# Expert weights found in groups of four, TensorE's expert products two steps later, in a hybrid decoder step

## The chip, the core and the metric

One core of a Trainium2 chip runs the whole program. The metric is the device time of one execution in microseconds (us). The engines are TensorE (PE in the profile; PEld is its weight load), VectorE (DVE), ScalarE (ACT), GpSimd (POOL) and SyncE (SP); SyncE and GpSimd issue the DMAs of this kernel, and 16 DMA engines carry them.

## The reference, cut to what matters

The program is one layer of a decoder for 512 prompt tokens and 8 running sequences. It has a modulated RMSNorm, a combined projection, gated-DeltaNet and forgetting attention, an output projection, and then PEER, a layer with 16384 experts of which each token and each of 8 heads picks 16. The change is in PEER alone, which computes this:

```
q = (xb @ wq).reshape(blk, PEER_HEADS, 2, PEER_DK_HALF)
s = jnp.einsum('thpc,hpnc->thpn', q, subkeys).astype(jnp.float32)
sv, si = lax.top_k(s, PEER_TOPK)
...
fv, fi = lax.top_k(cand, PEER_TOPK)
eidx = jnp.take_along_axis(cidx, fi, axis=-1)
gate = jax.nn.softmax(fv, axis=-1)
act = jax.nn.gelu(jnp.einsum('thkd,td->thk', pu[eidx], xb).astype(jnp.float32), approximate=False) * gate
return jnp.einsum('thk,thkd->td', act.astype(xb.dtype), pv[eidx])
```

So for each token, head and pick, a row of `pu` (1024 numbers) is multiplied with the token and summed, the sum goes through GELU and is scaled by the gate, and the row of `pv` (1024 numbers) times that weight is added to the token's output. The rows of `pu` and `pv` lie side by side in one table, `peer_uv`, 8 KB for an expert.

## The kernel before, in words

The expert stage starts at about 946 us of the span and lasts to its end. The prompt is cut into 4 tiles of 128 tokens, one token on each partition. A unit is one tile and one head (32 units, `UNITS`), and a step is one of the 16 picks of a unit; a further unit of 8 steps, `SAMPLES`, one for each running sequence, stands after unit 27. That makes 520 steps, listed in `steps_`. `events` is the loop that each engine writes out for itself: event e is step e for GpSimd's lookahead, VectorE and ScalarE, and TensorE does step e - `BEHIND` in it.

One step g goes through the engines like this:

- GpSimd, `gather(g)`, L2006: one indirect DMA brings 128 rows of 8 KB (1 MB, `u` and `v` of 128 experts) into buffer g % 8 of `UV`. Six of the 8 buffers lie in the tile RING, the last two in R, which is how the trace names them: the names alone tell which of the 8 steps a row belongs to. From `gather(8)` on, it waits for `v_used` to reach g - 7: TensorE must be through with step g - 8.
- VectorE, `dot(g)`, L1786 (L1784 for the samples): waits for the gather to land, multiplies `u` with the token's row `H2` and sums it (one instruction and the read of its accumulator).
- ScalarE, `gelu(q)`, L1098 (L1096): GELU over the dots of a group of steps, 128x2.
- VectorE, `weigh(q)`, L1804 (L1801): that times the gate, 128x2, which gives the semaphore `weights`.
- ScalarE, `diagonal(g)`, L1108: the identity scaled by the weight column, a 128x128 matrix in one of 4 places of `DG`; it waits for `weights`.
- TensorE, `value_step(g)`, L413: diagonal times `v`, two products 128x512, summed over a whole tile (8 units) in two PSUM banks. Its last matmul raises `v_used`. The samples (`sample_step`) need no diagonal: they multiply the matrix `AM`, whose columns `weigh` fills, with `v`.

All loops are written out, and each engine's queue is in the order of the program. In event e VectorE does `dot(e)`, then in even events `weigh` of steps e - 2 and e - 1, then some of the top-16 search of the unit after the next (`picks`), and here and there a norm. ScalarE in odd events does `gelu` of steps e - 1 and e, then the diagonals of steps e - 3 and e - 2. TensorE does `value_step(e - 4)` and then the slot of event e, if there is one.

Slots (`post_slots`, `slots_at`) are the other work of this stage: for tiles 1 to 3 the output projection (`wo`, two products 128x512 in a slot), the turning of the normed tokens (`turn`), the query projection (`wq`) and the scores. One slot goes with one event: they lie at events 56 to 109 (tile 1), 184 to 237 (tile 2) and 301 to 366 (tile 3, with the samples' rows). SyncE loads their weights, 2 MB at a time, in that region. Outside it TensorE has the expert products alone.

At the end of a tile, `sums_out` on VectorE (event 7 after the last step of the tile) waits for the last product of that tile.

Of the kernel before, what the change touches and what calls it, by code (L numbers as in the profile page):

```python
# [8 lines left out]
ALU = mybir.AluOpType  # L9
ACT = mybir.ActivationFunctionType  # L10
# [25 lines left out]
def hybrid_decoder_step(nc, a, o):  # L36

    ctx = ExitStack()
    with ctx:
        sems = {}  # L40

        def S(name):
            if name not in sems:
                sems[name] = ctx.enter_context(nc.semaphore(name))
            return sems[name]
# [24 lines left out]
        def part(_t, _at, _n, /, **dims):  # L70
            v = _t[:, _at:_at + _n]
            if not dims:
                return v
            names = list(dims)
            return v.rearrange(f"row ({' '.join(names)}) -> row {' '.join(names)}", **{k: dims[k] for k in names[1:]})
# [105 lines left out]
        GTT = R1[:, 11880:11888]  # L181
        DOTS = R1[:, 11888:11896]
        AM = R1[:, 11896:11960]
        EIX = R2[:, 11264:11328].bitcast(U32).rearrange("q (t n) -> q t n", t=4)
        FVS = part(R2, 11328, 64, t=4, n=16)
        DOT = part(R2, 11392, 64, t=4, n=16)
        AG = part(R2, 11456, 64, t=4, n=16)
        GAT = part(R2, 11520, 64, t=4, n=16)
# [88 lines left out]
        def take_bank(job, pool):  # L277

            n = taken[pool]
            taken[pool] += 1  # L280
            size = len(pools[pool])
            b = pools[pool][n % size]
            if n >= size:
                nc.tensor.wait_ge(S(f"bank{b}_free"), n // size)
            job_of[job] = (b, n // size + 1)
            newest[0] = job
            return banks[b]
# [104 lines left out]
        units = list(range(28)) + [SAMPLES] + list(range(28, UNITS))  # L392
        steps_ = [(n, s_) for n in units for s_ in range(NB if n == SAMPLES else STEPS)]
        at_step = {step_: g for g, step_ in enumerate(steps_)}
        AHEAD, BEHIND = 3, 4
        events = range(len(steps_) + BEHIND)

        def step_at(e):

            return steps_[e] if 0 <= e < len(steps_) else (None, None)  # L400

        def slots_of(e):

            n, s_ = step_at(e)
            return slots_at.get(n * STEPS + s_, ()) if n is not None and n < SAMPLES else ()
# [5 lines left out]
        def _(pe):  # L411
            def mm(out, lhsT, rhs, start=True, stop=True, sem=None, **k):
                i = nc.tensor.matmul(out, lhsT, rhs, start=start, stop=stop, **k)  # L413
                if sem is not None:
                    i.then_inc(sem, 1)
                return i
# [38 lines left out]
            for t in range(5):  # L455
                n = P if t < 4 else NB
# [409 lines left out]
                mm(hi[:, :], DG[:, k % 4, :], UV[g % UN][:, 1536:2048], first, last, S("v_used"))  # L866

            def sample_step(g, t):
                pe.wait_ge(S("weights"), g // 2 + 1)
                if t == 0:  # L870
                    take_bank(("ys", 0), "D")
                    take_bank(("ys", 1), "D")
                pe.wait_ge(S(f"uv_in{g % UN}"), 16 * (g // UN + 1))
                for half in range(2):
                    mm(banks[job_of["ys", half][0]][0:NB, :], AM[:, t * 8:t * 8 + 8], UV[g % UN][:, 1024 + half * 512:1536 + half * 512], t == 0, t == NB - 1,
                       S("v_used") if half else None)

            for e in events:
                g = e - BEHIND
                n, s_ = step_at(g)  # L880
# [14 lines left out]
        def _(act):  # L895
            A = nc.scalar.activation
# [9 lines left out]
            for t in range(5):  # L906
                n = P if t < 4 else NB
# [145 lines left out]
            def root(name, t):  # L1053
                n = P if t < 4 else NB
                act.wait_ge(S("sumsq"), nth_norm(name) + 1)
                A(SS[0:n, 5 + t:6 + t], SS[0:n, t:t + 1], ACT.Sqrt, scale=1.0 / D_MODEL, bias=EPSB[0:n, :]).then_inc(S("root"), 1)
# [31 lines left out]
            def gates(n):  # L1088
                act.wait_ge(S("picked"), n + 1)
                A(GAT[:, n % 4, :], FVS[:, n % 4, :], ACT.Exp, bias=NMX[:, n % 4:n % 4 + 1], accum_out=SUMG[:, n % 4:n % 4 + 1]).then_inc(S("gate_raw"), 1)  # L1090

            def gelu(q):
                n, s_ = steps_[2 * q]
                act.wait_ge(S("dots"), 2 * q + 2)
                if n == SAMPLES:
                    A(DOTS[:, s_:s_ + 2], DOTS[:, s_:s_ + 2], ACT.Gelu).then_inc(S("gelu"), 1)  # L1096
                else:
                    A(AG[:, n % 4, s_:s_ + 2], DOT[:, n % 4, s_:s_ + 2], ACT.Gelu).then_inc(S("gelu"), 1)  # L1098

            def diagonal(g):  # L1100
                n, s_ = steps_[g]
                if n == SAMPLES:
                    return
                k = n * STEPS + s_
                act.wait_ge(S("weights"), g // 2 + 1)
                if k >= 4:
                    act.wait_ge(S("v_used"), at_step[divmod(k - 4, STEPS)] + 1)
                A(DG[:, k % 4, :], ident[:, :], ACT.Copy, scale=AG[:, n % 4, s_:s_ + 1]).then_inc(S("diagonal"), 1)  # L1108
# [20 lines left out]

            for e in events:  # L1130
                n, s_ = step_at(e)
                if e % 2:
                    if n is not None:
                        gelu(e // 2)
                    for g in (e - 3, e - 2):
                        if 0 <= g < len(steps_):
                            diagonal(g)
                if n is not None and n + 1 < UNITS and s_ == 6:
                    gates(n + 1)
                if n is not None and n % PH == 0 and 0 < n < SAMPLES and s_ == 9:  # L1140
                    root(f"f{n // PH - 1}", n // PH - 1)
                if (n, s_) == (29, 9):
                    root("f4", 4)
                if (n, s_) == (25, 6):
                    act.wait_ge(S("sample_picks"), 1)
                    A(GT64[0:64], FV64[0:64], ACT.Exp, bias=MX64[0:64], accum_out=SUM64[0:64]).then_inc(S("sample_exp"), 1)
                for slot_ in slots_of(e - 1):
                    post_slot(*slot_)
# [4 lines left out]
        def _(dve):  # L1153
            V = nc.vector
# [614 lines left out]
            def unit_picks(n):  # L1769

                if n + 2 < UNITS:
                    yield from prompt_picks(n + 2)
                if n == 24:
                    yield from sample_picks()
# [20 lines left out]

            def weigh(q):

                n, s_ = steps_[2 * q]
                dve.wait_ge(S("gelu"), q + 1)
                if n == SAMPLES:  # L1800
                    V.tensor_tensor(AM[:, 9 * s_:9 * s_ + 10:9], DOTS[:, s_:s_ + 2], GTT[:, s_:s_ + 2], ALU.mult).then_inc(S("weights"), 1)  # L1801
                else:
                    ag = AG[:, n % 4, s_:s_ + 2]
                    V.tensor_tensor(ag, ag, GAT[:, n % 4, s_:s_ + 2], ALU.mult).then_inc(S("weights"), 1)  # L1804

            def sums_out(t):

# [64 lines left out]
            for e in events:  # L1872
                n, s_ = step_at(e)
                if n is not None:
                    dot(e)
                if e % 2 == 0 and 0 <= e // 2 - 1 < len(steps_) // 2:
                    weigh(e // 2 - 1)
                if n is not None and n < SAMPLES:
                    if s_ == 4:
                        for _ in picking:  # L1880
                            pass
                        picking = unit_picks(n)
                    for _ in range(2 if 0 <= n * STEPS + s_ - 24 * STEPS - 4 < STEPS else 1):
                        next(picking, None)
                    if s_ == 8 and n + 1 < UNITS:
                        gate_scale(n + 1)
                    if n and n % PH == 0:
                        if s_ == 6:
                            sums_out(n // PH - 1)
                        elif s_ == 7:  # L1890
                            residual(n // PH - 1)
                        elif s_ == 11:
                            finish(n // PH - 1)
                    if n == 25 and s_ == 8:
                        sample_gates()
                    if n == 26 and s_ == 4:
                        sample_indices()
                    if n == 29:
                        if s_ == 6:
                            sample_sums()  # L1900
                        elif s_ == 7:
                            residual(4)
                        elif s_ == 11:
                            finish(4)
                for slot_ in slots_of(e - 1):
                    post_slot(*slot_)
# [449 lines left out]
```

## Time and profile before

| what | value |
|---|---|
| time, median of 3 runs | 2443.9 us (2438.39 to 2452.11) |
| time of the profiled execution | 2435.51 us |
| its span | 2433.2 us |
| TensorE matmul busy | 1916.3 us, 79% |
| VectorE busy | 1415.4 us, 58% |
| ScalarE busy | 502.3 us, 21% |
| GpSimd busy | 866.0 us, 36% |
| DMA rate in the expert stage | 364 to 420 GB/s in the slices of the page, but for the last |

The span runs from the first to the last instruction; the profiled execution's own time has 2.3 us around it. In a row of the timeline the columns are: start in us, duration in us, engine, line, operation, tile written and tile read, shapes, how many instructions were merged, and in brackets how long the engine was idle before them and what ended that.

### The profile page before, as it was taken

How to read it: one execution, taken by the hardware profiler on the slowest of the kernel's cores; microseconds unless marked ns; L12 is line 12 of the kernel's file. 1: busy time of each engine (PE TensorE's matmuls, PEld its weight loads, DVE VectorE, ACT ScalarE, POOL GpSimd, SP SyncE). 2: the span in 40 equal slices, each digit the busy share in tenths (PEclk: the TensorE clock that was granted, in tenths of full speed). 3: DMA queues.
4: the chain of work that ended last, by engine and by line, in shares of the span. 5: the costliest groups of instructions: out<-in, count | busy, mean ns of one | idle time of the engine just before them, and what ended most of it. 6: DMA issues, size and time to landing. Idle time of an engine off the chain costs nothing.

```text
span 2433.2 us, 24921 instructions
## 1 busy us (share of the span) xinstructions
PE 1916.3 (79%) x7976; PEld 1050.7 (43%) x7976; DVE 1415.4 (58%) x3274; ACT 502.3 (21%) x1312; POOL 866.0 (36%) x642
## 2 busy tenths in 40 slices
PE   2799976785899887778886778886788997776776
PEld 1364433454777766323552323542232552222222
DVE  2200686668555524676656776656776667865764
ACT  0111211111212112222221222222222222211221
POOL 0000263795123201343443443334443344443442
PEclk6789985556999998899999899999999999999999
DMA  7022342764345457999999999999999999999997
GB/s 283 18 70 75 123 163 65 231 198 158 105 139 174 156 179 272 366 420 406 416 415 409 398 413 402 416 416 415 393 408 364 383 410 416 388 417 420 397 380 294
DMA packets 168930, 728.32 MB, mean 299 GB/s; under 512 B 17789, under 2 KB 18782, under 8 KB 102098
## 3 DMA queue, kind: packets, MB, share of 16 engines
q0 software_dynamic: 75024, 545.82, 55.1%
q1 hardware_dynamic: 93778, 180.92, 21.9%
q8 instruction: 65, 1.06, 0.2%
q14 instruction: 63, 0.52, 0.1%
HBM read 720.69 MB, written 6.08 MB: 299 GB/s over the span
## 4 chain that ended last, share of the span: by engine, by line
PE 41%; DMA 31%; DVE 13%; issue 6%; POOL 4%; ACT 2%; SPq 2%; another core or an unknown queue 0%; DVEq 0%; ACTq 0%; POOLq 0%
PE bank L413 39%; DMA RING<-in_peer_uv,R 20%; DMA R<-in_peer_uv,R 8%; DVE RING L1786 3%; SPq L2020 1%; POOL R L1934 1%; PE bank L420 1%; DVE R L1786 1%; ACT R L1108 1%; DMA R<-h2s_d 1%; DVE RING L1319 1%; POOL MV L1934 1%; DMA R<-in_x_sample 1%; POOL R L1951 0%; DMA R<-in_x_prompt 0%
## 5 line engine op out<-in xcount | busy, mean ns | idle before, releaser
L413 PE MATMUL bank<-RING,R 128*128 128x512 f32 (+1 forms) x1560 | 756.0, 625 | 227.0 <-ACT R L1108 217.1
L2006 POOL DMA_INDIRECT RING<-in_peer_uv,R x390 | 439.3, 1126 | 759.5 <-PE bank L413 653.0
L413 PE MATMUL bank<-R 128*128 128x128 f32 (+5 forms) x2248 | 491.3, 372 | 95.4 <-ACT R L1108 68.0
L413 PEld LDWEIGHTS bank<-RING,R 128*128 128x128 f32 (+1 forms) x1560 | 287.5, 195 | 629.8 <-issue 616.7
L413 PEld LDWEIGHTS bank<-R 128*128 128x128 f32 (+2 forms) x2248 | 302.1, 194 | 253.4 <-issue 226.8
L1786 DVE SCALAR_TENSOR_TENSOR RING<-RING,R 128x1024 f32<-128x1024 f32 x192 | 235.0, 1225 | 172.5 <-DMA RING<-in_peer_uv,R 171.8
L1786 DVE SCALAR_TENSOR_TENSOR RING<-RING,MV 128x1024 f32<-128x1024 f32 x192 | 235.0, 1224 | 155.3 <-DMA RING<-in_peer_uv,R 153.5
L1098 ACT ACTIVATE R<-R 128x2 f32<-128x2 f32 x256 | 52.1, 203 | 1051.4 <-DVE RING L1786 844.6
L2006 POOL DMA_INDIRECT R<-in_peer_uv,R x130 | 149.1, 1147 | 204.8 <-PE bank L413 200.7
L1108 ACT ACTIVATE R<-ident,R 128x128 f32<-128x128 f32 x512 | 173.6, 386 | 0.5 <-PE bank L413 0.2
L420 PE MATMUL bank<-ident,R 128*128 128x128 f32 (+2 forms) x310 | 64.0, 351 | 137.1 <-ACT R L996 54.5
L413 PEld LDWEIGHTS bank<-HT,R 128*128 128x128 f32 x1024 | 134.7, 197 | 47.0 <-issue 45.9
L1984 POOL TENSOR_TENSOR R<-R,level 128x512 f32<-128x512 f32 x56 | 80.1, 1453 | 198.3 <-DVEq L1601 144.0
L413 PE MATMUL bank<-HT,RING 128*128 128x512 f32 (+1 forms) x336 | 150.5, 602 | 0.0
L413 PE MATMUL bank<-HT,R 128*128 128x128 f32 (+1 forms) x1024 | 135.7, 282 | 0.7 <-issue 0.7
L1786 DVE SCALAR_TENSOR_TENSOR R<-R,MV 128x1024 f32<-128x1024 f32 x64 | 78.4, 1225 | 66.9 <-DMA R<-in_peer_uv,R 66.5
L1934 POOL TENSOR_TENSOR R<-R,RING 128x2048 f32<-128x2048 f32 x20 | 90.5, 4532 | 73.3 <-DMA R<-in_cache_k 73.1
L420 PEld LDWEIGHTS bank<-ident,R 128*128 128x128 f32 (+2 forms) x310 | 49.0, 188 | 154.6 <-ACT R L996 57.3
L1786 DVE SCALAR_TENSOR_TENSOR R<-R 128x1024 f32<-128x1024 f32 x64 | 78.2, 1223 | 60.3 <-DMA R<-in_peer_uv,R 60.2
L413 PE MATMUL bank<-RING,HT 128*8 128x128 f32 (+5 forms) x768 | 111.2, 352 | 2.1 <-ACT HT L1050 2.1
L413 PE MATMUL bank<-R,HT 128*128 128x64 f32 (+2 forms) x288 | 96.0, 478 | 3.1 <-DVE HT L1378 3.1
L1927 POOL DMA_INDIRECT RING<-in_cache_logf,small x1 | 1.3, 1289 | 269.1 <-PE bank L413 269.1
(295 smaller groups left out, 1820.8 us busy)
## 6 DMA issues: line engine op xcount, KB each, us to landing
R<-in_peer_wq SPq DMA_DIRECT2D x16, 2048.0 KB
RING<-in_w_mod SPq DMA_DIRECT2D x12, 2048.0 KB, 8.3
R<-in_cache_v SPq DMA_DIRECT2D x84, 256.0 KB, 3.2
R<-in_cache_k SPq DMA_DIRECT2D x80, 256.0 KB, 4.0
MV<-in_cache_k SPq DMA_DIRECT2D x48, 256.0 KB, 3.6
R<-in_w_out SPq DMA_DIRECT2D x6, 2048.0 KB
MV<-in_cache_v SPq DMA_DIRECT2D x44, 256.0 KB, 3.2
RING<-in_w_in SPq DMA_DIRECT2D x5, 2048.0 KB, 8.6
```

What stands on the lines that cost most here:

```text
L413: i = nc.tensor.matmul(out, lhsT, rhs, start=start, stop=stop, **k)
L420: i = nc.tensor.transpose(out, in_, ident[0:n, 0:n])
L1098: A(AG[:, n % 4, s_:s_ + 2], DOT[:, n % 4, s_:s_ + 2], ACT.Gelu).then_inc(S("gelu"), 1)
L1108: A(DG[:, k % 4, :], ident[:, :], ACT.Copy, scale=AG[:, n % 4, s_:s_ + 1]).then_inc(S("diagonal"), 1)
L1319: V.tensor_reduce(SC[:, :, n // 4, (n % 4) * 4:(n % 4) * 4 + 4].rearrange("p h g -> p g h"), pages(n).rearrange("p g (h d) -> p g h d", d= ...
L1786: V.scalar_tensor_tensor(u, u, 1.0, H2[n // PH % 2], ALU.mult, ALU.mult, accum_out=DOT[:, n % 4, s_:s_ + 1]).then_inc(S("dots"), 1)
L1927: nc.gpsimd.indirect_dma_start(LG, None, a["cache_logf"][0].rearrange("n p h -> n (p h)"), bass.IndirectOffsetOnAxis(ap=PTI, axis=0)).then ...
L1934: T(k, k, QB[:, n // 4 % 2:n // 4 % 2 + 1, :].to_broadcast([P, 4, 512]), ALU.mult).then_inc(S("kprod"), 1)
L1984: T(M, AT, level[:, lv:lv + 1, :].to_broadcast([P, 4, P]), ALU.mult).then_inc(S(f"level{hb}"), 1)
L2006: nc.gpsimd.indirect_dma_start(UV[g % UN], None, a["peer_uv"][0], bass.IndirectOffsetOnAxis(ap=idx, axis=0)).then_inc(S(f"uv_in{g % UN}"), 16)
L2020: sp.dma_start(dst, src, **k).then_inc(S(sem), 16)
```

## The change

GELU, gate product and diagonals go in groups of four steps (`GROUP = 4`) in place of two. The gelu of steps 4q to 4q+3 stands in ScalarE's event 4q+3, the `weigh` of that group in VectorE's event 4q+4 behind `dot(4q+4)`, and the four diagonals in ScalarE's event 4q+5. `BEHIND` is 6 in place of 4, so TensorE's `value_step(g)` stands in event g + 6, behind the slots of events up to g + 5. The number of `UV` buffers (8) and of `DG` places (4), and all that the other engines do, stay.

```diff
--- before.py
+++ after.py
@@ -392,7 +392,8 @@
         units = list(range(28)) + [SAMPLES] + list(range(28, UNITS))
         steps_ = [(n, s_) for n in units for s_ in range(NB if n == SAMPLES else STEPS)]
         at_step = {step_: g for g, step_ in enumerate(steps_)}
-        AHEAD, BEHIND = 3, 4
+        AHEAD, BEHIND = 3, 6
+        GROUP = 4
         events = range(len(steps_) + BEHIND)
 
         def step_at(e):
@@ -866,7 +867,7 @@
                 mm(hi[:, :], DG[:, k % 4, :], UV[g % UN][:, 1536:2048], first, last, S("v_used"))
 
             def sample_step(g, t):
-                pe.wait_ge(S("weights"), g // 2 + 1)
+                pe.wait_ge(S("weights"), g // GROUP + 1)
                 if t == 0:
                     take_bank(("ys", 0), "D")
                     take_bank(("ys", 1), "D")
@@ -1090,19 +1091,19 @@
                 A(GAT[:, n % 4, :], FVS[:, n % 4, :], ACT.Exp, bias=NMX[:, n % 4:n % 4 + 1], accum_out=SUMG[:, n % 4:n % 4 + 1]).then_inc(S("gate_raw"), 1)
 
             def gelu(q):
-                n, s_ = steps_[2 * q]
-                act.wait_ge(S("dots"), 2 * q + 2)
+                n, s_ = steps_[GROUP * q]
+                act.wait_ge(S("dots"), GROUP * q + GROUP)
                 if n == SAMPLES:
-                    A(DOTS[:, s_:s_ + 2], DOTS[:, s_:s_ + 2], ACT.Gelu).then_inc(S("gelu"), 1)
+                    A(DOTS[:, s_:s_ + GROUP], DOTS[:, s_:s_ + GROUP], ACT.Gelu).then_inc(S("gelu"), 1)
                 else:
-                    A(AG[:, n % 4, s_:s_ + 2], DOT[:, n % 4, s_:s_ + 2], ACT.Gelu).then_inc(S("gelu"), 1)
+                    A(AG[:, n % 4, s_:s_ + GROUP], DOT[:, n % 4, s_:s_ + GROUP], ACT.Gelu).then_inc(S("gelu"), 1)
 
             def diagonal(g):
                 n, s_ = steps_[g]
                 if n == SAMPLES:
                     return
                 k = n * STEPS + s_
-                act.wait_ge(S("weights"), g // 2 + 1)
+                act.wait_ge(S("weights"), g // GROUP + 1)
                 if k >= 4:
                     act.wait_ge(S("v_used"), at_step[divmod(k - 4, STEPS)] + 1)
                 A(DG[:, k % 4, :], ident[:, :], ACT.Copy, scale=AG[:, n % 4, s_:s_ + 1]).then_inc(S("diagonal"), 1)
@@ -1129,10 +1130,10 @@
 
             for e in events:
                 n, s_ = step_at(e)
-                if e % 2:
-                    if n is not None:
-                        gelu(e // 2)
-                    for g in (e - 3, e - 2):
+                if e % GROUP == GROUP - 1 and n is not None:
+                    gelu(e // GROUP)
+                if e % GROUP == 1:
+                    for g in range(e - 5, e - 1):
                         if 0 <= g < len(steps_):
                             diagonal(g)
                 if n is not None and n + 1 < UNITS and s_ == 6:
@@ -1795,13 +1796,13 @@
 
             def weigh(q):
 
-                n, s_ = steps_[2 * q]
+                n, s_ = steps_[GROUP * q]
                 dve.wait_ge(S("gelu"), q + 1)
                 if n == SAMPLES:
-                    V.tensor_tensor(AM[:, 9 * s_:9 * s_ + 10:9], DOTS[:, s_:s_ + 2], GTT[:, s_:s_ + 2], ALU.mult).then_inc(S("weights"), 1)
+                    V.tensor_tensor(AM[:, 9 * s_:9 * s_ + 28:9], DOTS[:, s_:s_ + GROUP], GTT[:, s_:s_ + GROUP], ALU.mult).then_inc(S("weights"), 1)
                 else:
-                    ag = AG[:, n % 4, s_:s_ + 2]
-                    V.tensor_tensor(ag, ag, GAT[:, n % 4, s_:s_ + 2], ALU.mult).then_inc(S("weights"), 1)
+                    ag = AG[:, n % 4, s_:s_ + GROUP]
+                    V.tensor_tensor(ag, ag, GAT[:, n % 4, s_:s_ + GROUP], ALU.mult).then_inc(S("weights"), 1)
 
             def sums_out(t):
 
@@ -1873,8 +1874,8 @@
                 n, s_ = step_at(e)
                 if n is not None:
                     dot(e)
-                if e % 2 == 0 and 0 <= e // 2 - 1 < len(steps_) // 2:
-                    weigh(e // 2 - 1)
+                if e % GROUP == 0 and 0 <= e // GROUP - 1 < len(steps_) // GROUP:
+                    weigh(e // GROUP - 1)
                 if n is not None and n < SAMPLES:
                     if s_ == 4:
                         for _ in picking:
```

## Rows read from the trace of the kernel before

**Rows 1.** The page: busy time of the engines, and the chain of waits.

```profile
PE 1916.3 (79%) x7976; PEld 1050.7 (43%) x7976; DVE 1415.4 (58%) x3274; ACT 502.3 (21%) x1312; POOL 866.0 (36%) x642
...
PE 41%; DMA 31%; DVE 13%; issue 6%; POOL 4%; ACT 2%; SPq 2%; another core or an unknown queue 0%; DVEq 0%; ACTq 0%; POOLq 0%
```

**Rows 2.** Busy time by window: the five stretches without slots.

```profile
core 0: us, PE busy (x) PEld busy (x) DVE busy (x) ACT busy (x) POOL busy (x), PEclk, DMA share, GB/s
1011.10:1112.50 101.40, 76.16 (x162) 29.92 (x161) 69.50 (x189) 24.65 (x72) 42.65 (x40) 0.97 1.01 416
1283.00:1474.70 191.70, 140.34 (x288) 55.20 (x287) 130.13 (x351) 46.04 (x131) 81.11 (x72) 0.95 1.00 407
1644.80:1804.90 160.10, 115.02 (x240) 45.30 (x239) 109.24 (x295) 38.35 (x109) 67.14 (x60) 0.96 1.00 407
2012.30:2221.30 209.00, 151.29 (x324) 59.16 (x323) 154.04 (x433) 49.59 (x145) 86.22 (x80) 0.98 0.99 410
2271.60:2407.80 136.20, 99.38 (x210) 39.45 (x209) 84.61 (x203) 29.27 (x89) 60.05 (x52) 0.96 0.99 403
```

**Rows 3.** The same view: the query slots of tiles 1 to 3, and tile 3's output slots.

```profile
1164.50:1283.00 118.50, 102.20 (x428) 61.26 (x428) 71.06 (x196) 26.36 (x87) 49.30 (x40) 1.00 1.02 415
1499.50:1644.80 145.30, 124.19 (x497) 71.98 (x496) 89.57 (x239) 36.50 (x109) 57.49 (x49) 1.00 1.02 415
1897.30:2012.30 115.00, 108.53 (x476) 66.43 (x475) 71.09 (x197) 29.47 (x92) 48.55 (x41) 1.00 1.01 407
1804.90:1897.30 92.40, 82.41 (x200) 31.15 (x199) 61.11 (x152) 24.10 (x60) 30.27 (x27) 0.96 0.94 361
```

**Rows 4.** Timeline: one round of the buffers where nothing else runs.

```profile
2377.95 1.23 DVE L1786 SCALAR_TENSOR_TENSOR RING<-RING,MV 128x1024 f32<-128x1024 f32 x1 [1.26 <-DMA RING<-in_peer_uv,R]
2379.10 0.16 DVE L1804 TENSOR_TENSOR R<-R 128x2 f32<-128x2 f32 x1
2380.42 1.23 DVE L1786 SCALAR_TENSOR_TENSOR RING<-RING,MV 128x1024 f32<-128x1024 f32 x1 [1.16 <-DMA RING<-in_peer_uv,R]
2381.69 0.20 ACT L1098 ACTIVATE R<-R 128x2 f32<-128x2 f32 x1 [4.17 <-DVE RING L1786]
2381.80 0.68 ACT L1108 ACTIVATE R<-ident,R 128x128 f32<-128x128 f32 x2
2382.33 3.67 PE L413 MATMUL bank<-R 128*128 128x512 f32 x8 [1.29 <-ACT R L1108]
2384.55 0.94 POOL L2006 DMA_INDIRECT R<-in_peer_uv,R  x1 [2.10 <-PE bank L413]
...
2392.84 1.23 DVE L1786 SCALAR_TENSOR_TENSOR R<-R,MV 128x1024 f32<-128x1024 f32 x1 [1.25 <-DMA R<-in_peer_uv,R]
```

**Rows 5.** Timeline: a round whose gather was issued late.

```profile
2350.77 0.68 ACT L1108 ACTIVATE R<-ident,R 128x128 f32<-128x128 f32 x2
2351.30 8.89 PE L413 MATMUL bank<-RING,R 128*128 128x512 f32 x16 [2.75 <-ACT R L1108]
2354.84 1.81 POOL L2006 DMA_INDIRECT RING<-in_peer_uv,R  x1 [4.62 <-PE bank L413]
2363.04 1.23 DVE L1786 SCALAR_TENSOR_TENSOR RING<-RING,MV 128x1024 f32<-128x1024 f32 x1 [2.25 <-DMA RING<-in_peer_uv,R]
```

**Rows 6.** Timeline: the long wait at a turn slot, and the gather behind it.

```profile
1887.11 0.59 PE L420 MATMUL bank<-ident,R 8*128 8x8 f32 x4 [7.25 <-DVE R L1216]
1891.54 0.94 POOL L2006 DMA_INDIRECT RING<-in_peer_uv,R  x1 [10.48 <-PE bank L413]
1897.27 1.23 DVE L1786 SCALAR_TENSOR_TENSOR RING<-RING,R 128x1024 f32<-128x1024 f32 x1 [3.54 <-DMA RING<-in_peer_uv,R]
```

**Rows 7.** Timeline: the first two gate products of the samples.

```profile
2231.58 0.16 DVE L1801 TENSOR_TENSOR R<-R 128x2 f32<-128x2 f32 x1
2240.72 0.16 DVE L1801 TENSOR_TENSOR R<-R 128x2 f32<-128x2 f32 x1
```

## The prediction

> **What bounds the kernel now.** I read the page first, for shares: no engine is full, and the chain of waits is mostly TensorE and DMA [rows 1]. Then the busy time by window, because the expert stage has two kinds of stretch. Without slots [rows 2] the DMA share is 0.99 to 1.01 at 403 to 416 GB/s, while TensorE is busy three quarters of the time: there the kernel moves bytes. With query slots TensorE is at 85 to 94% and the DMA share is still 1.01 or 1.02; only in tile 3's output slots does the rate fall, to 361 GB/s [rows 3]. Then the timeline of one quiet round, for what keeps the DMA queue filled [rows 4]. The reader is to see a ring there, not a list of busy engines: dot, gelu, diagonals, products, gather, landing, dot.
>
> The ring in numbers [rows 4]. The dot at 2380.42 is the last that the gelu of 2381.69 waits for; the diagonals start at 2381.80 (1.38 us after the dot's start), the products at 2382.33, and the first product done lets a gather go at 2384.55 (2.75 after the diagonals). It goes into a buffer named R, and the first dot on R is at 2392.84, 8.29 later. 1.38 + 2.75 + 8.29 = 12.42 us. How many steps is that? The first diagonal of a pair (step 2q) waits for the dot of step 2q+3, because ScalarE's next gelu stands before it, and it frees the buffer of step 2q+8. So the ring covers five steps: 12.42 / 5 = 2.484 us a step, 1.0486 MB in that time being 422 GB/s. That is the DMA rate; the ring follows it, with slack.
>
> How much slack? A late round shows it [rows 5]: that gather's instruction took 1.81 in place of 0.94 us, started at 2354.84, and its dot came at 2363.04, after VectorE had waited 2.25 us where 1.16 to 1.26 is usual [rows 4], so it was about 1.0 late. 8.20 less the 0.87 of the long instruction is 7.33 us: this is what a gather needs when the queue before it has only just run short. Of the 8.29 of a quiet round about 1 us is waiting in the queue. With the queue wholly run out (GpSimd idle 10.48 before) it took 1897.27 - 1891.54 = 5.73 [rows 6].
>
> **The change: the ring gets shorter by a step.** Step 4q is now weighed behind the dot of step 4q+4, and it frees the buffer of step 4q+8. From dot to dot that is four steps, not five, and the budget at the DMA rate falls from 12.42 to 4 x 2.484 = 9.94 us. What must fit in it: the dot and the gate product behind it, 2379.26 - 2377.95 = 1.31 [rows 4], and about 0.14 to the diagonal, 1.45 in all; gelu is off this path, since it needs dot 4q+3 only. Then 2.75 to the gather; then the landing. With the landing of a quiet round, 8.29, that is 12.5; with 7.33, 11.5; with 5.73, 9.93. So the gather of step 4q+8 comes late once in four steps in all cases but the last. The other three are released 1.8 us apart (3.67 for two steps) where the DMA takes 2.48 for each, so they follow without a gap: one gap in each group.
>
> **TensorE's pauses.** Four steps of products are 2 x 3.67 = 7.3 us in one burst; in a round of 9.94 or more TensorE then has 2.6 us or more of idle time in one piece, where it now has 1.29 twice [rows 4]. The row with 2.75 idle before it has 16 matmuls in 8.89 us in place of 7.3, and its diagonals-to-gather time is 2354.84 - 2350.77 = 4.07, not 2.75 [rows 5]; the granted clock of these stretches is 0.95 to 0.98 [rows 2], so it does fall from 2.4 to 1.2 GHz at times. The ring at the low clock is 1.45 + 4.07 + landing: 11.25 with 5.73, 12.85 with 7.33.
>
> The Trainium skill, "TensorE: Matmul & The Clock Gate", section "Why this matters for your kernels", says to leave no idle gaps between bursts of matmuls, since the clock then goes back to half. That speaks against this change, and the trace agrees in the row with 2.75 idle before it; applied to every burst, the rule is what the second rival supposes.
>
> Which value? Bounds of the round are 9.93 and 12.85. I take the low clock at the start of most bursts (4.07) and a landing of 6.2, between 5.73 and 7.33, because the queue now runs partly out in each round and so comes nearer to the row with the empty queue: 1.45 + 4.07 + 6.2 = 11.7 us a group of four.
>
> The Trainium skill, "DMA: Bandwidth & Descriptors", section "Anatomy of one DMA — SWDGE (gpsimd) path", gives 2.0 us plus the bytes at 436 GB/s for one DMA of this kind, an estimate of 4.4 us for 1 MB. With that the ring would be shorter than 9.94 and nothing would be lost. The rows show 5.73 at the least, so the measurement decides; this is the reason for the third rival.
>
> How many groups? The five stretches without slots are steps 16 to 55, 112 to 183, 240 to 299, 368 to 447 and 464 to 515: 304 steps, 76 groups, and they now last 798.4 us (the five windows' lengths) [rows 2], 10.5 a group; the 0.56 above 9.94 is weight loads and late dots. 76 x 11.7 = 889: plus 91. Ends: 76 x 12.85 = 977, plus 178; and 0 at the other.
>
> **Elsewhere.** Query slots (128 steps, 378.8 us, 11.8 a group) [rows 3]: products and slots alternate, TensorE is nearly full and a ring of 11.7 just fits; where no weights are being loaded it doesn't, so between 0 and 1 us for each of 32 groups; I take half, 15. Tile 3's output slots (28 steps in 92.4 us) [rows 3] are TensorE's own work and don't change. At the samples' turn slot TensorE waits 7.25 us [rows 6]; it has passed two products fewer before that slot, so two gathers fewer are under way: 0 to 5 us, I take 4. Samples: their first four products now wait for the dot of sample 4, whose gate product is at 2240.72 today, where the first pair goes at 2231.58 [rows 7]; the gathers behind them start some 8 us later, but VectorE there waits for the sample rows anyway: 0 to 8, I take 3. Nothing from the 130 gate products that go (0.16 each) and the gelus: VectorE waits over 1 us for DMA in each quiet step [rows 4], and ScalarE is idle 79% [rows 1]. The end of the kernel costs nothing: today's last four products already wait for the last dots. `sums_out` stands seven events behind its last step and TensorE six, so it hardly waits; SyncE's queue waits for dots and norms, which move with the rest, and no instruction of it is moved.
>
> Sum: 2435.5 (the profiled execution) + 91 + 15 + 4 + 3 = 2548.5. The median of the runs shown is 8.4 above that execution, so 2557; I say 2556.
>
> **The rivals.** First, the clock holds: 1.45 + 2.75 + 6.5 = 10.7 a group, plus 15 and perhaps 12 elsewhere, 2471 (before's median plus 27). For it: a gap of 2.6 is not above the 2.75 that fell. Against: any late landing makes the gap longer than 2.75. Chance 0.2.
>
> Second, low clock in every burst and no easing of the landing: 12.85 a group, plus 178 and 22, 2644. Against: an emptier queue landed in 5.73. Chance 0.12.
>
> Third, the ring still fits: landing 5.73 at the full clock, 9.93 against 9.94. Then the round stays at the DMA rate and the time is 2444, no change. It decides at one point: whether VectorE's waits ahead of the dot of step 4q+8 stay at 1.2 us. Chance 0.08.
>
> Fourth, the other side, faster: with the products two steps later, TensorE can begin a slot two events sooner, while it would be idle. In two steps it is idle 1.29 [rows 4]; if each of the three blocks of slots gained that and its waits (7.25 at the longest [rows 6]) shrank, 5 to 15 us would go, 2434. It needs the third as well, since otherwise the ring eats it. Chance 0.05.
>
> **How the numbers follow.** 0.55 for the forecast (2500 to 2610), and the rest as above. Within 0.5% (12 us) is what a measurement of this kernel can't tell from no change: 0.08; faster 0.05; slower 0.87. The range of 8 in 10 is 2468 to 2630: it takes in the first rival and stops short of the bound of 2644.
>
> **What would show it.** In the changed kernel's quiet stretches: one VectorE wait of 2 to 3.5 us in every four dots and three of 1.2; ScalarE's copies in fours every 11 to 12 us; TensorE in bursts of 16 matmuls with 3 to 4 us between them; a DMA rate near 360 GB/s where it is 403 to 416; granted clock clearly below 0.95. Wrong would be: dots still 2.48 apart through a group, or a longer time with the extra in the slot stretches.

## The result and the profile after

The changed kernel takes 2614.6 us (median of 4 runs, 2606.89 to 2615.35), the kernel before 2443.4 in the same comparison: a ratio of 1.0696, 95% interval 1.066 to 1.0732. The profiled execution took 2615.3 us, 179.8 more than that of before.

The page, its busy times and its chain of waits:

```profile
PE 1992.6 (76%) x7976; PEld 1093.9 (42%) x7976; DVE 1409.8 (54%) x3144; ACT 489.1 (19%) x1182; POOL 857.9 (33%) x642
...
PE 40%; DMA 32%; DVE 13%; issue 7%; POOL 3%; ACT 2%; SPq 2%; another core or an unknown queue 0%; DVEq 0%; POOLq 0%; ACTq 0%
```

Against [rows 1], VectorE and ScalarE have 130 instructions fewer each, and the time did not fall for it. TensorE has the same 7976 matmuls and is busy 76 us more: the same work, more of it at the lower clock. The shares of the chain have hardly moved, so they alone wouldn't say what went wrong.

The busy time by window does. First the five stretches without slots (the same steps as in [rows 2]), with their sum:

```profile
1013.10:1132.70 119.60, 84.11 (x163) 34.88 (x164) 68.74 (x179) 23.73 (x62) 45.93 (x40) 0.86 0.91 350
1321.10:1539.90 218.80, 155.49 (x288) 63.88 (x289) 129.36 (x332) 44.38 (x113) 79.02 (x71) 0.84 0.91 347
1725.10:1910.10 185.00, 127.84 (x243) 52.81 (x244) 108.41 (x279) 36.97 (x94) 69.94 (x60) 0.84 0.91 347
2131.50:2376.00 244.50, 169.52 (x322) 69.56 (x322) 152.72 (x413) 47.64 (x125) 89.15 (x80) 0.87 0.91 350
2432.20:2586.20 154.00, 107.64 (x208) 44.22 (x208) 84.06 (x189) 28.11 (x76) 58.76 (x52) 0.89 0.91 352
sum 921.90, PE 644.60 PEld 265.34 DVE 543.29 ACT 180.82 POOL 342.80; mean PE 128.92 PEld 53.07 DVE 108.66 ACT 36.16 POOL 68.56
```

The DMA rate is 347 to 352 GB/s where it was 403 to 416, and the clock 0.84 to 0.89 where it was 0.95 to 0.98. The stretches last 921.9 us in place of 798.4: 123.5 of the 179.8 us are here.

The DMA share, 0.91, has fallen less than the rate. Summed over the five stretches, the DMA engines were busy for some 840 us where some 797 were enough before for about the same bytes. So of the 123.5 us they stood idle in some 81, and for some 42 more the same work took them longer.

Then the query slots of the three tiles and tile 3's output slots, as in [rows 3]:

```profile
1187.80:1321.10 133.30, 108.22 (x416) 63.77 (x416) 70.39 (x186) 25.36 (x77) 45.03 (x40) 0.92 0.98 380
1568.80:1725.10 156.30, 127.59 (x488) 74.47 (x488) 88.54 (x227) 35.18 (x97) 52.53 (x49) 0.93 0.98 388
2012.40:2131.50 119.10, 105.97 (x457) 63.90 (x455) 70.61 (x187) 27.12 (x81) 46.06 (x41) 1.00 1.00 388
1910.10:2012.40 102.30, 86.45 (x215) 34.24 (x214) 60.78 (x144) 24.01 (x54) 28.72 (x28) 0.92 0.88 331
```

The query slots last 408.7 us in place of 378.8, tile 3's output slots 102.3 in place of 92.4.

The timeline of one round, which answers to [rows 4]. The four gathers at the top are those of one group; the first of them is the second row.

```profile
2557.07 1.23 DVE L1787 SCALAR_TENSOR_TENSOR RING<-RING,MV 128x1024 f32<-128x1024 f32 x1 [1.25 <-DMA RING<-in_peer_uv,R]
2557.66 1.44 POOL L2007 DMA_INDIRECT RING<-in_peer_uv,R  x1 [6.26 <-PE bank L414]
2559.41 0.94 POOL L2007 DMA_INDIRECT RING<-in_peer_uv,R  x1 [0.30 <-PE bank L414]
2561.09 0.94 POOL L2007 DMA_INDIRECT R<-in_peer_uv,R  x1 [0.75 <-PE bank L414]
2562.81 0.94 POOL L2007 DMA_INDIRECT R<-in_peer_uv,R  x1 [0.78 <-PE bank L414]
2563.67 1.23 DVE L1787 SCALAR_TENSOR_TENSOR RING<-RING,MV 128x1024 f32<-128x1024 f32 x1 [2.90 <-DMA RING<-in_peer_uv,R]
2564.82 0.16 DVE L1805 TENSOR_TENSOR R<-R 128x4 f32<-128x4 f32 x1
2565.01 1.28 ACT L1109 ACTIVATE R<-ident,R 128x128 f32<-128x128 f32 x4 [4.01 <-DVE R L1805]
2565.56 7.10 PE L414 MATMUL bank<-RING,R 128*128 128x512 f32 x16 [3.02 <-ACT R L1109]
2567.20 1.23 DVE L1787 SCALAR_TENSOR_TENSOR RING<-RING,MV 128x1024 f32<-128x1024 f32 x1 [2.22 <-DMA RING<-in_peer_uv,R]
2567.78 1.45 POOL L2007 DMA_INDIRECT RING<-in_peer_uv,R  x1 [4.04 <-PE bank L414]
...
2574.64 1.23 DVE L1787 SCALAR_TENSOR_TENSOR RING<-RING,MV 128x1024 f32<-128x1024 f32 x1 [1.27 <-DMA RING<-in_peer_uv,R]
...
2576.53 5.37 PE L414 MATMUL bank<-RING,R 128*128 128x512 f32 x8 [3.87 <-ACT R L1109]
```

The dot at 2563.67 is that of step 4q+4. Behind it comes the gate product, and only then do the four scale copies (the diagonals, ScalarE's four merged instructions) run. The gather at 2567.78 brings step 4q+8, whose dot is at 2574.64: 10.97 us for four steps in this good round, where 9.94 is the DMA rate. VectorE's waits of 2.90 and 2.22 us show where the queue had run short, and TensorE stood still for 3.02 us in one piece, then for 3.87; behind the second pause 8 matmuls took 5.37 us, where 3.67 is the high clock [rows 4].

### The profile page after: what moved, and what is told of

Read it like the earlier page. It is cut to its first block, busy times and chain, and to the rows that moved or that the text cites. A ratio compares the mean times of both kernels' runs of the same rounds, so it can differ in the third digit from the quotient of the medians.

```text
span 2612.9 us, 24661 instructions
## 1 busy us (share of the span) xinstructions
PE 1992.6 (76%) x7976; PEld 1093.9 (42%) x7976; DVE 1409.8 (54%) x3144; ACT 489.1 (19%) x1182; POOL 857.9 (33%) x642
## 4 chain that ended last, share of the span: by engine, by line
PE 40%; DMA 32%; DVE 13%; issue 7%; POOL 3%; ACT 2%; SPq 2%; another core or an unknown queue 0%; DVEq 0%; POOLq 0%; ACTq 0%
PE bank L414 38%; DMA RING<-in_peer_uv,R 27%; DVE RING L1787 5%; DMA R<-in_peer_uv,R 2%; ACT R L1109 2%; SPq L2021 1%; POOL R L1935 1%; PE bank L421 1%; DVE RING L1320 1%; POOL MV L1935 1%; DMA R<-h2s_d 1%; DMA R<-in_x_sample 0%; POOL R L1952 0%; POOL R L1951 0%; DMA R<-in_x_prompt 0%
## 5 line engine op out<-in xcount | busy, mean ns | idle before, releaser
L414 PE MATMUL bank<-RING,R 128*128 128x512 f32 (+1 forms) x1560 | 838.0, 687 | 389.0 <-ACT R L1109 372.5
L414 PEld LDWEIGHTS bank<-RING,R 128*128 128x128 f32 (+1 forms) x1560 | 325.9, 219 | 832.1 <-issue 813.8
L414 PE MATMUL bank<-R 128*128 128x128 f32 (+6 forms) x2248 | 485.8, 369 | 28.3 <-ACT R L1071 9.0
L414 PEld LDWEIGHTS bank<-R 128*128 128x128 f32 (+3 forms) x2248 | 302.7, 193 | 169.3 <-issue 143.5
L1109 ACT ACTIVATE R<-ident,R 128x128 f32<-128x128 f32 x512 | 164.6, 390 | 451.5 <-DVE R L1805 434.0
L2007 POOL DMA_INDIRECT R<-in_peer_uv,R x130 | 142.4, 1096 | 143.0 <-PE bank L414 135.3
L1099 ACT ACTIVATE R<-R 128x4 f32<-128x4 f32 x128 | 26.3, 205 | 812.0 <-DVE RING L1787 436.2
L414 PEld LDWEIGHTS bank<-HT,RING 128*128 128x128 f32 (+1 forms) x336 | 62.4, 191 | 80.5 <-issue 80.5
```

The source lines that it names most:

```text
L1099: A(AG[:, n % 4, s_:s_ + GROUP], DOT[:, n % 4, s_:s_ + GROUP], ACT.Gelu).then_inc(S("gelu"), 1)
L2007: nc.gpsimd.indirect_dma_start(UV[g % UN], None, a["peer_uv"][0], bass.IndirectOffsetOnAxis(ap=idx, axis=0)).then_inc(S(f"uv_in{g % UN}"), 16)
```

## The experiments

Two rivals were set against the theory that the ring, from a dot to the dot on the buffer that it frees, is a step shorter: A, TensorE's place behind more slots does it; B, the bursts of 16 matmuls and the low clock behind each pause do it. Ratios are to runs of the kernel before on the same chip, whose own median moved between 2429 and 2443 us; "quiet" is the length of the five stretches without slots in the profiled execution.

**The other half of the change alone.**

```
-        AHEAD, BEHIND = 3, 4
+        AHEAD, BEHIND = 3, 6
```

> The kernel before with BEHIND = 6 and groups of two left as they were: only TensorE's place in the order of the slots moves. Theory (the ring of the buffers is shortened from five steps to four by the group of four): the ring stays at five steps, so the time stays within 0.5% of before, 2431 to 2455 us. Rival A (the order does it: products behind two more slots keep the buffers back): 2490 to 2600 us. Rival B (bursts of four and TensorE's clock): as the theory, 2431 to 2455.

Measured: 2454.0 us, ratio 1.0062 (1.0037 to 1.0087). Quiet 796.8 us against 798.4. The later products cost 0.6%, a little more than the 0.5% that the theory allowed, all of it in the stretches with slots: query slots 387.6 us against 378.8, the blocks with output and turn slots (steps 56 to 71, 184 to 191 and 300 to 327) 179.8 against 169.2. A small cost that the theory had at nothing; rival A is out for the rest.

**The groups of four alone**: the changed kernel with `BEHIND = 4`.

> The changed kernel with BEHIND = 4: groups of four alone. Theory: all of the loss is still there, 2595 to 2630 us. Rival A (the order): most of it goes, 2444 to 2520. Rival B (bursts and clock): 2595 to 2630.

Measured: 2621.9 us, ratio 1.0743 (1.0684 to 1.0802), quiet 922.9. The grouping carries the whole loss. The two halves don't add up: once the group of four is there, the later products cost nothing more. By stretch (one profiled execution of each) the three blocks with output and turn slots take 183.9 us here, 179.8 with the later products alone and 186.3 with both, against 169.2 before; the query slots take 420.8 here and 408.7 with both.

**The group of four, weighed a dot earlier.** One edit to the changed kernel on VectorE:

```
-                if e % GROUP == 0 and 0 <= e // GROUP - 1 < len(steps_) // GROUP:
-                    weigh(e // GROUP - 1)
+                if e % GROUP == GROUP - 1 and e // GROUP < len(steps_) // GROUP:
+                    weigh(e // GROUP)
```

> The changed kernel, but VectorE does the gate product of a group right behind the group's own last dot (4q+3) instead of behind dot 4q+4; bursts of four, BEHIND = 6 and 8 buffers stay. Theory: the ring is five steps again, 12.42 us at the DMA rate, against some 1.7 + 2.75 to 4.1 + 5.6 to 7.3 = 10 to 13 needed, so most of the loss goes: 2440 to 2500 us, the quiet stretches near 2.5 to 2.6 us a step. Rival B (bursts of 16 matmuls and the low clock behind each pause do it, whichever dot is waited for): the bursts and pauses stay, so 2560 to 2615. Rival A: 2595 to 2630.

Measured: 2479.3 us, ratio 1.0168 (1.0114 to 1.0223), quiet 809.7. Bursts, groups, buffers and `BEHIND` are those of the changed kernel, and 112 of the 123 us are gone. Its five windows:

```profile
1008.80:1110.00 101.20, 79.93 (x167) 33.15 (x166) 69.66 (x181) 23.57 (x63) 44.31 (x40) 0.93 1.01 417
1283.90:1474.50 190.60, 142.49 (x289) 59.09 (x288) 130.69 (x333) 43.92 (x112) 80.12 (x71) 0.91 1.00 403
1657.10:1818.20 161.10, 124.88 (x245) 51.25 (x244) 109.43 (x279) 36.81 (x94) 70.60 (x60) 0.88 0.99 399
2035.80:2254.00 218.20, 162.30 (x321) 66.48 (x320) 154.71 (x412) 47.34 (x125) 90.38 (x81) 0.88 0.98 394
2309.20:2447.80 138.60, 107.66 (x210) 44.22 (x210) 84.72 (x189) 28.62 (x78) 58.26 (x52) 0.88 0.99 395
```

The clock is still down, 0.88 to 0.93, and the DMA rate is nearly back, 394 to 417 GB/s against 403 to 416. So the clock fell here and took at most the remaining 11 us with it, against rival B.

**Pairs, weighed early.** In the kernel before:

```
-                if e % 2:
-                    if n is not None:
-                        gelu(e // 2)
-                    for g in (e - 3, e - 2):
+                if e % 2 and n is not None:
+                    gelu(e // 2)
+                if e % 2 == 0:
+                    for g in (e - 2, e - 1):
...
-                if e % 2 == 0 and 0 <= e // 2 - 1 < len(steps_) // 2:
-                    weigh(e // 2 - 1)
+                if e % 2 == 1 and e // 2 < len(steps_) // 2:
+                    weigh(e // 2)
```

> The kernel before, groups of two and BEHIND = 4, with the gate product right behind the pair's own last dot and the diagonals in ScalarE's next event, ahead of the next gelu: the ring becomes seven steps long (from dot 2q+1 to dot 2q+8). Theory: before's quiet stretches, 2.6 us a step where 2.484 is the DMA rate, lose nearly all their gaps: 2385 to 2430 us. Rival B: bursts and pauses are as before, 2431 to 2455. Rival (VectorE's short wait for gelu, some 0.4 us a pair, costs): 2450 to 2500.

Measured: 2410.3 us, ratio 0.9887 (0.9835 to 0.9939), quiet 778.3: 1.1% below the kernel before, with the whole interval under 1. The price of weighing early is in its timeline, a wait of VectorE of 0.27 us for the gelu, beside waits for DMA that it shortens:

```profile
2364.57 1.22 DVE L1786 SCALAR_TENSOR_TENSOR RING<-RING,MV 128x1024 f32<-128x1024 f32 x1 [1.25 <-DMA RING<-in_peer_uv,R]
2365.84 0.20 ACT L1098 ACTIVATE R<-R 128x2 f32<-128x2 f32 x1 [3.85 <-DVE RING L1786]
2366.08 0.16 DVE L1804 TENSOR_TENSOR R<-R 128x2 f32<-128x2 f32 x1 [0.27 <-ACT R L1098]
2366.27 0.69 ACT L1108 ACTIVATE R<-ident,R 128x128 f32<-128x128 f32 x2 [0.23 <-DVE R L1804]
2367.06 1.23 DVE L1786 SCALAR_TENSOR_TENSOR R<-R,MV 128x1024 f32<-128x1024 f32 x1 [0.82 <-DMA R<-in_peer_uv,R]
```

**The ring shortened without any group of four.** The kernel before with one buffer fewer:

```
-        UV = [part(FLAT, i * 2048, 2048) for i in range(6)] + [part(R1, 12288, 2048), part(R2, 8192, 2048)]
+        UV = [part(FLAT, i * 2048, 2048) for i in range(6)] + [part(R1, 12288, 2048)]
```

> The kernel before, groups of two and BEHIND = 4, with seven buffers in place of eight: the ring of the first step of each pair is four steps long, as in the changed kernel, without the bursts of four. Theory: 1.38 + 2.75 + 7.0 to 7.4 = 11.1 to 11.5 us for four steps against 9.94, so 76 groups x 0.7 to 1.0 above before's 10.5 and some more in the query slots: 2490 to 2550 us, quiet stretches at 2.8 to 2.9 us a step. Rival B (bursts and clock): 2431 to 2470.

Measured: 2611.9 us, ratio 1.0707 (1.0647 to 1.0767), above the 2490 to 2550 that the theory gave. Two of its five windows with the sum line of all five, and of its timeline one late pair:

```profile
1313.20:1534.70 221.50, 149.09 (x288) 58.17 (x287) 130.39 (x351) 46.04 (x131) 76.75 (x72) 0.92 0.94 350
2127.90:2374.50 246.60, 168.47 (x320) 65.72 (x319) 154.40 (x433) 49.59 (x145) 87.26 (x80) 0.90 0.92 347
...
sum 923.80, PE 638.86 PEld 249.14 DVE 548.34 ACT 187.89 POOL 329.34; mean PE 127.77 PEld 49.83 DVE 109.67 ACT 37.58 POOL 65.87
```

```profile
2561.29 3.67 PE L413 MATMUL bank<-RING,R 128*128 128x512 f32 x8 [1.23 <-ACT R L1108]
2561.84 1.23 DVE L1786 SCALAR_TENSOR_TENSOR R<-R,MV 128x1024 f32<-128x1024 f32 x1 [1.22 <-DMA R<-in_peer_uv,R]
2563.51 0.93 POOL L2006 DMA_INDIRECT RING<-in_peer_uv,R  x1 [2.10 <-PE bank L413]
2566.19 1.23 DVE L1786 SCALAR_TENSOR_TENSOR RING<-RING,MV 128x1024 f32<-128x1024 f32 x1 [3.05 <-DMA RING<-in_peer_uv,R]
```

The quiet stretches last 923.8 us, those of the changed kernel 921.9: with pairs, bursts of 8 matmuls and the rest of the program as before, a ring of four steps costs the same. (The clock is not as before: it fell to 0.87 to 0.92 here too, and the fillers below tell what that is worth.) The row to see is VectorE's wait of 3.05 us where [rows 4] has 1.16 to 1.26. This is the strongest evidence for the theory. What it missed is the size. Its sum was 1.38 + 2.75 + 7.0 to 7.4, 11.1 to 11.5 us; the means over the rounds of the trace are 1.38, 3.26 from scale copy to gather, 0.17 of longer gather instructions and 7.47, 12.27 in all. So about half of the miss lies between scale copy and gather, and the rest in the landing and the gather instruction.

**The group of four with the step given back.** The changed kernel with a ninth buffer, laid over constants that are dead in this stage and the rest of the weight ring:

```
+        BIG = sb("BIG", [P, 3 * KT * SLOTW + 13 * P])
...
+        RING = BIG[:, 0:3 * KT * SLOTW].rearrange("p (s n) -> p s n", s=3)
...
-        UV = [part(FLAT, i * 2048, 2048) for i in range(6)] + [part(R1, 12288, 2048), part(R2, 8192, 2048)]
+        UV = [part(FLAT, i * 2048, 2048) for i in range(6)] + [part(R1, 12288, 2048), part(R2, 8192, 2048), BIG[:, 6 * 2048:7 * 2048]]
```

> The changed kernel with a ninth buffer (made of constants that are dead in the expert stage and the ring's rest): the group of four, the wait for dot 4q+4 and the bursts stay, and the ring is five steps again. Theory: 12.42 us against 1.34 + 3.9 + 5.6 to 7 = 10.8 to 12.2 needed: 2445 to 2500 us. Rival B (bursts and clock whatever the ring): 2560 to 2615.

Measured: 2457.4 us, ratio 1.0073 (1.0042 to 1.0104), quiet 813.9, with granted clocks of 0.87 to 0.92. Group, bursts and the wait for dot 4q+4 are there, and of the loss there 108 of 123.5 us are gone.

**The ninth buffer in the kernel before.**

> The kernel before with the ninth buffer alone: the ring is six steps, 14.9 us. Theory: between before and the kernel with the early gate product (seven steps, 2410): 2405 to 2430 us. Rival (before has slack enough, and the early gate product gained in another way): 2436 to 2450, no change.

Measured: 2412.0 us, ratio 0.9877 (0.9826 to 0.9927), quiet 783.2, as the theory gave: a longer ring gains 1.2% without any early gate product.

**TensorE kept busy in its pause.** In the changed kernel, matmuls whose result nobody reads, ahead of the first product of 64 of the 130 groups (60 of the 76 in the quiet stretches):

```
+            def keep_busy(x):
+                last = max((j for j in job_of if job_of[j][0] == 7), key=lambda j: job_of[j][1])
+                job_read(pe, last)
+                for _ in range(x):
+                    mm(banks[7][:, :].rearrange("p (m c) -> p m c", m=4), ident[:, :], level[:, 0:4, :])
...
+                if g % GROUP == 0 and any(a_ <= e < b_ for a_, b_ in ((16, 56), (112, 184), (242, 300), (370, 416), (486, 522))):
+                    keep_busy(3)
```

> The changed kernel with three matmuls of a constant by the identity, 128x512, whose result nobody reads, ahead of the first product of each group of four in the stretches without slots (some 61 groups of them): they fill TensorE's pause, so that the burst begins at the high clock. All of the reference's work is kept. In the changed kernel diagonals to gather takes 3.88 us on average in these stretches where 2.75 is the row at the high clock. Theory (ring of four steps, of which the clock is one term): that term goes back to about 2.8, the landing takes a part of it back as the queue is less empty (6.9 to 7.4), so 0.6 to 1.1 us for each of the groups: 2545 to 2580 us, still far above before. Rival B (the clock is all of it): 2444 to 2490. Rival (the clock is not on the path): 2600 to 2620.

Measured: 2601.7 us, ratio 1.065 (1.0588 to 1.0712): hardly a gain. The theory's own 2545 to 2580 was missed, and the time lies in the range of the third reading, in which the clock is not on the path. Quiet 913.5, clock 0.91 to 0.94. Since the clock was only half mended, the same with five fillers:

> As the kernel with three filler matmuls ahead of each group of four, but with five (4.3 us at the high clock): the pause is filled whole, all of the reference's work is kept. With three, the granted clock in the quiet stretches went from 0.84 to 0.89 up to 0.91 to 0.94 and the time only from 2614.6 to 2601.7 us, because the landing took back what the products gave. Theory now (the landing gives way to whatever comes before it, and only dots, products and buffers together set the ring): clock near 1.0, diagonals to gather about 2.9, time 2585 to 2615 us. Rival (the clock was only half mended by three, and its price comes back once it is whole): 2530 to 2575.

Measured: 2598.9 us, ratio 1.0723 (1.0677 to 1.0769), quiet 912.9. Its windows:

```profile
1007.40:1125.20 117.80, 115.94 (x267) 49.64 (x265) 68.88 (x180) 23.73 (x62) 46.48 (x41) 1.00 0.96 363
1305.10:1516.60 211.50, 202.88 (x461) 88.05 (x462) 129.32 (x333) 44.39 (x113) 78.69 (x71) 0.98 0.96 364
1699.00:1880.50 181.50, 168.88 (x384) 72.76 (x384) 108.28 (x280) 36.96 (x94) 68.99 (x60) 0.99 0.94 356
2105.60:2350.60 245.00, 202.11 (x440) 84.83 (x438) 152.79 (x413) 47.64 (x125) 92.14 (x80) 0.95 0.92 350
2404.80:2561.90 157.10, 133.39 (x297) 56.60 (x298) 84.21 (x190) 28.13 (x76) 62.38 (x53) 0.98 0.94 352
```

The clock is at 0.95 to 1.00, where before's is 0.95 to 0.98, and the DMA rate is still 350 to 364 GB/s. The two intervals and that of the changed kernel overlap; by the quiet stretches the clock is worth some 9 us of the 123. In the first three, where 40 of the 43 groups have fillers, it is 12.6 us of 70.2 (453.2 before, 523.4 changed, 510.8 here); in the last two, where 20 of 33 have them, nothing comes back (398.5 changed, 402.1 here). The DMA engines were idle for some 55 us in place of 82 and busy for some 858 in place of 840: most of what the sooner gathers filled was used up by slower transfers. Rival B is out as the main cause; the two kernels with groups of four and a ring of five steps are still 11 and 16 us above before there, which may be its share.

**Is it the ring, or the number of buffers?** The early pairs with seven buffers:

> The kernel with the early gate product, pairs and BEHIND = 4, with seven buffers: the ring is six steps, as in the kernel before with nine. Seven buffers in the kernel before cost 7%. Theory (the length of the ring counts, from the dot that is waited for to the dot on the freed buffer, not the number of buffers): 2405 to 2430 us. Rival (seven buffers are too few for the DMA engines by themselves): 2520 to 2610.

Measured: 2419.3 us, ratio 0.996 (0.994 to 0.998), quiet 782.1. Seven buffers cost 7% where the ring is four steps, and 0.7% (0.996 against 0.989) where it is six; some 4 of the 11 us between the two profiled executions are in the quiet stretches.

**The best of it.** Early pairs with `BEHIND = 2`:

> The kernel with the early gate product (pairs, eight buffers, 2410 us) with BEHIND = 2 in place of 4. BEHIND = 6 alone cost 0.6%, all of it in the stretches with slots. Theory (products that stand behind fewer slots free buffers sooner, and the quiet stretches don't care): 5 to 15 us less than with 4, 2395 to 2406. Rival (TensorE's slots now wait for the dots, as two steps are all that lies between): 2410 to 2440.

Measured: 2404.3 us, ratio 0.9905 (0.9874 to 0.9936), not told apart from `BEHIND = 4` (0.9887). With the ninth buffer as well:

> The same with the ninth buffer as well: the ring is eight steps. Theory: the quiet stretches are at the DMA rate already (778 us in place of 755 for 304 steps at 2.484), so at most 10 us more than with eight buffers: 2385 to 2405. Rival (more buffers still buy time, as DMA takes more at once): 2360 to 2385.

Measured: 2397.2 us, ratio 0.9873 (0.9842 to 0.9904), the lowest time of all, though its interval overlaps those of the other early pairs. Quiet 783.2: a ring of eight steps has nothing over six.

All kernels by the length of the shortest ring, in steps from the dot that is waited for to the dot on the freed buffer:

| ring | kernels | quiet stretches, us | ratio |
|---|---|---|---|
| 4 | changed; group of four alone; seven buffers; fillers 3 and 5 | 921.9; 922.9; 923.8; 913.5 and 912.9 | 1.065 to 1.074 |
| 5 | before; `BEHIND = 6`; group of four weighed early; with nine buffers | 798.4; 796.8; 809.7; 813.9 | 1; 1.006; 1.017; 1.007 |
| 6 | before with nine buffers; early pairs with seven | 783.2; 782.1 | 0.988; 0.996 |
| 7 | early pairs, with `BEHIND` 4 and 2 | 778.3; 786.2 | 0.989; 0.991 |
| 8 | early pairs, nine buffers, `BEHIND = 2` | 783.2 | 0.987 |

## Why the prediction was right, point by point

The forecast was 2556 us, a loss of 112; measured were 2614.6, a loss of 171, in the upper part of the range of 2468 to 2630. The mechanism was the one forecast, and its size was set too low by a third.

**The ring gets a step shorter: right, and shown.** It was shown from both sides: shortened without the group of four (quiet stretches of 923.8 us), and given back with the group of four by two different edits (809.7 and 813.9). One detail was off: I expected one late dot and three on time. Over all groups of the quiet stretches the dots of a group came 3.83, 2.88, 2.77 and 2.66 us after the one before, so the first is late by most, and the others a little too.

**The size of the round: 12.1 us in place of 11.7.** 921.9 us over 76 groups are 12.13, against 10.5 before; the loss there is 123.5 us where 91 stood. Read from the trace over 75 rounds of the changed kernel, from the dot of step 4q+4 to that of step 4q+8: dot to scale copy 1.34 us (forecast 1.45), scale copy to gather 3.88 (4.07), long gather instruction 0.20 (not counted), landing 6.86 (6.2). Those add up to 12.29. The term that was mis-sized is the landing: I had let it sink towards the 5.73 of an empty queue, and it did so only in part. With the long instructions that the sum left out it is 0.86 too small, and the other two terms were 0.30 too large.

**TensorE's clock: seen rightly, priced wrongly.** The pauses and the fall of the clock came as foretold, 0.84 to 0.89. But "1.45 + 4.07 + 6.2" treats the terms as independent, and they aren't. With the five fillers scale copy to gather is 3.26 in place of 3.88 and the landing 7.40 in place of 6.86; the round is 12.08 in place of 12.29 (means of the rounds in the trace). With seven buffers it is 3.26, 7.47 and 12.27. (The fillers did not hold the products back: the median from scale copy to gather is 2.78 with them, 4.22 without.) A gather issued sooner took longer to land, so the low clock cost some 0.1 to 0.3 us a round by these runs, where the sum gave it 4.07 - 2.75 = 1.32. By the same token the first rival, that the clock holds and the round is 10.7, was wrong in kind: in the fillers' run the clock mostly holds, and the round is 12.08.

The Trainium skill, "TensorE: Matmul & The Clock Gate", section "Why this matters for your kernels", warns of idle gaps between bursts; the trace agrees on the clock, 0.84 to 0.89 in the changed kernel's stretches, and the run with fillers shows that little of the time hung on it here.

**Elsewhere: 56 us where 22 stood.** Query slots plus 29.9 (forecast 15): a ring of four steps doesn't fit there in most groups, at 12.7 us by the same reading. The three blocks with output slots plus 17.1 (forecast 4 at one turn slot, nothing else): the prediction took tile 3's output slots [rows 3] for TensorE's own work that doesn't change, and that step was wrong: the later products alone add 10.6 in these blocks, the group of four alone 14.7, and the seven buffers alone 13.5, each in its own run. Samples plus 6.0 (forecast 3). The rest, 3 us, lies in the start and the end.

**What hid the removed work: right as far as is seen.** VectorE and ScalarE have fewer instructions in every kernel with groups of four, and none of them beat the kernel before. No run took the instructions out with the ring as it was.

**The rival with no change and the one on the faster side: wrong, but near a true one.** Both needed a ring that fits, 9.93 us against 9.94, and it took 12.1. The gain lay in the other direction, a longer ring by weighing earlier; before's own quiet stretches had 20 us to give.

**Open.** Why a gather that comes late behind others lands in 6.9 to 7.5 us on average, where one into an empty queue takes 5.5 to 5.8. A ring of four steps came to 12.1 to 12.3 us in every kernel, whatever the products did, as if the four gathers of a round had a floor of their own; nothing here tells what holds it there. The DMA records show where the time goes, not why. One 8 KB packet of the gathers took 0.319 us on average in before's quiet stretches and 0.341 to 0.349 with rings of four steps (changed, seven buffers, five fillers); with five steps and groups of four it was 0.324. So the transfers themselves are slower where the queue runs short. No run puts the release off by known times, which would tell more.

## What to carry to other kernels

Count a ring of buffers in steps, from the wait that ends last to the use of the buffer that it frees, and set its budget (steps times the time of a step) against its latency; grouping small instructions lengthens the first member's wait, and one step is enough to fall off. Here 12.42 us of budget against some 11.5 needed was within some 1% of the best ring, 9.94 cost 7%, and no time was seen to come back from the small instructions saved. Where a result is needed to free a buffer, put its short consumer right behind the producer, even at a wait of 0.27 us: that was 1.1% faster than the kernel before.

## What the runs showed of the hardware

- TensorE's clock fell from 2.4 to 1.2 GHz for a while behind a pause of 3.87 us (granted clock 0.76 from 2576.5 to 2578.2 us) and in [rows 5] behind one of 2.75 (0.65 from 2351.3 to 2353), yet held behind one of 3.02 (1.00 over its 16 matmuls, 7.10 us): the length of the pause alone doesn't settle it. Matmuls whose result nobody reads kept it up (0.95 to 1.00), which gave back some 9 us in the quiet stretches.
- One indirect gather of 1 MB took 5.5 to 5.8 us from its instruction to the dot with nothing ahead of it, and 6.9 to 7.5 on average when it came late behind others. In a queue that never ran short it depends on what stands ahead: 8.29 in [rows 4], 13.1 on average for the first of a pair with early pairs.
- With rings of four steps the DMA engines were busy 5 to 9% longer in the quiet stretches (some 840 to 865 us against 797) for about the same bytes.
- The gather's instruction on GpSimd, mostly 0.94 us, was 1.44 and 1.45 us in two of the six gather rows above, and 1.81 in [rows 5].
